# Slot tables of a grouped mixture of experts: the token products move from VectorE to GpSimd, and VectorE makes the one-hots of both halves before its gate products

## The chip, the cores and the metric

The kernel runs on one core of one Trainium2 chip. The metric is the device time of one launch in microseconds, lower is better. The median of the runs is compared, and the profile comes from one execution of its own.

## What is computed

One decoder layer over 2048 tokens of width 1024: a mixer (four mLSTM heads beside gated short convolutions), a LayerNorm, a mixture of sixteen experts with two chosen per token, and a second LayerNorm. The edit is in the mixture. The reference sorts the (token, expert) pairs by expert and lets each expert work on its own rows:

```python
flat_e = expert_idx.reshape(-1)
order = jnp.argsort(flat_e)
tok_sorted = order // TOP_K
gate_sorted = gates.reshape(-1)[order]
...
y = y_buf[dest] * gate_sorted[:, None].astype(x.dtype)
return jnp.zeros_like(xf).at[tok_sorted].add(y).reshape(b, s, d)
```

## The kernel before

The program has four stages, one behind the other with a barrier of all engines between them: the mixer, the router, the experts, the last normalisation. The edit is at the head of the expert stage (the function `experts`).

The router leaves for each of the 4096 pairs (2048 tokens, first and second choice) its expert column, its rank within the expert and its gate. A pair is a place in a tile of 128 partitions x 32: 16 tiles of tokens for the first choice and 16 for the second, which are the two **halves** of this text. From these the expert stage makes **slot tables**: for each of 48 table columns (three for each expert, of 128, 128 and 32 rows) and each of 128 rows, which token sits there, and with what gate. That is a sum over all pairs, and TensorE makes it: for each of the 32 places n, the one-hot of the row (`LOH[:, n]`, 128 wide) is multiplied with `RH[:, n]`, which is 96 wide: the one-hot of the column times the token's number plus one in `RH[:, n, 0]`, and the same one-hot times the gate in `RH[:, n, 1]`. Each fp32 product shows as two passes in the profile, so there are 64 of them (L1680), all added into one PSUM bank.

What VectorE does for that, in `one_hots`, after some short operations on the ranks, is for each half:

1. the column table, `RH[:, half, 1]`: column numbers against a number per pair (L1536), 128x768
2. the row one-hot, `LOH[:, half]` (L1538), 128x2048
3. the token product into `RH[:, half, 0]` (L1541), 128x768
4. the gate product, in place in `RH[:, half, 1]` (L1544), 128x768, which raises `oh_done`

TensorE waits for `oh_done` before place 0 and before place 16. Then VectorE splits the first slice of the first expert's weights (`split_gu(r, 0)`, L1476) and in `tables` reads the sums out of PSUM (L1551 on): the gather rows, which release GpSimd's indirect DMAs of the token rows (L1334), and later the scatter rows. TensorE transposes the gathered rows (L1628), ScalarE and VectorE split them, and the first expert's gate and up products start (L1612).

Each engine has its own queue, written out by hand; what an engine does is in the order of the code. `own.step` counts an operation of VectorE, and `own.wait` waits for all counted ones. `wait_apart` is a wait followed by a carrier that raises another semaphore. GpSimd has nothing between the router's end and the first gather. A loop `Fori(0, n_rounds)` encloses all; it runs once for these inputs. `DVE_TURN` is the number of counted operations in one turn.

Of the kernel before, what the change touches and what calls it, by code (L numbers as in the profile page):

```python
# [7 lines left out]
P = 128  # L8
# [4 lines left out]
ALU = mybir.AluOpType  # L13
# [10 lines left out]
def tensors(nc, ctx, stage):  # L24

    def sb(name, shape, dt=F32):
        return ctx.enter_context(nc.sbuf_tensor(f"{stage}_{name}", shape, dt))

    def ps(name, shape, dt=F32):
        return ctx.enter_context(nc.psum_tensor(f"{stage}_{name}", shape, dt))  # L30

    def sem(name):
        return ctx.enter_context(nc.semaphore(f"{stage}_{name}"))

    return sb, ps, sem


def wait_apart(engine, carrier, sem, value):


    engine.wait_ge(sem, value)
    engine.sem_inc(carrier, 1)
# [28 lines left out]
def mixer(nc, keep, x, w_in, b_in, conv_w, mh_g, w_out, ln_g, ln_b, x1_dram, acc_dram, alpha):  # L71
# [52 lines left out]
    with ctx:  # L124
# [357 lines left out]

        DVE_TURN = 61

        @block.vector
        def _(dve):
            own = Order(dve, dve_own, DVE_TURN)

# [155 lines left out]
            with dve.Fori(0, NG) as g:  # L644
# [88 lines left out]
                for t in range(NT):  # L733
                    dve.scalar_tensor_tensor(out=R[:, t], in0=R[:, t], scalar=lmv[:, t, 0:1], in1=lng[:],
                                             op0=ALU.subtract, op1=ALU.mult).then_inc(ln_gained, 1)
            assert own.n == DVE_TURN, own.n

# [494 lines left out]
def experts(nc, keep, x1_dram, acc_dram, w_gate, w_up, w_down):  # L1232
    D = x1_dram.shape[1]
    NE, _, F = w_gate.shape
    KC = D // P
    FC = F // P
    RING = 3
    NPAIR = keep.pair_rank.shape[1]
    TILES = NPAIR // 2
    NCOL = COLS * NE  # L1240
# [8 lines left out]
    with ctx:  # L1249
        sb, ps, sem = tensors(nc, ctx, "moe")  # L1250
# [11 lines left out]
        slot_f = sb("slot_parts", [P, 2, NPAIR])  # L1262
# [9 lines left out]
        LOH = keep.conv_or_residual[:, 0:NPAIR * P].rearrange("p (n s) -> p n s", s=P)  # L1272
        RH = X[:].rearrange("p k n -> p (k n)")[:, 0:NPAIR * 2 * NCOL].rearrange("p (n a b) -> p n a b", a=2, b=NCOL)
# [11 lines left out]
        dn_h, dn_l = sem("down_high_ready"), sem("down_low_ready")  # L1285
        a_used, b_used, u_used = sem("down_used_by_a"), sem("down_used_by_b"), sem("down_used_by_u")
        oh_done, s_ps = sem("one_hots_ready"), sem("slots_in_psum")
        last_taken, last_ps = sem("last_slots_taken"), sem("last_slots_in_psum")
        gather_ready, scatter_ready = sem("gather_rows_ready"), sem("scatter_rows_ready")
        x_in = [sem(f"x_rows_in{k}") for k in range(COLS)]  # L1290
# [6 lines left out]
        ended, idle = sem("round_ended"), sem("wait_carrier")  # L1297
# [3 lines left out]
        def trips(engine):  # L1301

            return engine.value_load(keep.rounds[0:1, 0:1], min_val=1, max_val=keep.most_rounds)
# [7 lines left out]
        @block.sync  # L1311
        def _(sp):
            n_rounds = trips(sp)
            with sp.Fori(0, n_rounds) as r:
                def load(e, w):
                    sp.wait_ge(gu_l, r * (NE * FC) + e * FC)
                    load_gate_up(sp, keep, w_gate[w], w_up[w])
                    wait_apart(sp, idle, dn_l, r * (NE * 2) + 2 * e)
                    sp.wait_ge(u_used, r * NE + e)
                    load_down(sp, keep, w_down[w])  # L1320

                for e in range(1, NE):
                    load(e, e)
                again = n_rounds - 1 - r
                with sp.If(again):
                    load(NE, 0)
                all_ended(sp, r)

        @block.gpsimd
        def _(pool):  # L1330
            def gather(r, e, k):

                n = ROWS[k]
                pool.indirect_dma_start(out=X[0:n, k], out_offset=None, in_=x1_dram,  # L1334
                                        in_offset=bass.IndirectOffsetOnAxis(
                                            ap=gather_i[0:n, COLS * e + k:COLS * e + k + 1], axis=0))\
                    .then_inc(x_in[k], 16)

            def gather_next(r, e, k):
                if e + 1 < NE:  # L1340
                    wait_apart(pool, idle, x_ps[k], r * NE + e + 1)
                    gather(r, e + 1, k)

            def scatter(r, e, k):
                n = COLS * e + k
                if n:
                    wait_apart(pool, idle, added, r * (NCOL * 16) + n * 16)
                if k == U:
                    wait_apart(pool, idle, yu_done, r * NE + e + 1)
                    to, rows, index = acc_dram.rearrange("s (q n) -> (s q) n", q=QUARTERS), YU[:], last_i[:, e:e + 1]  # L1350
                else:
                    for done in (y_act, y_dve):
                        wait_apart(pool, idle, done, r * (2 * NE) + 2 * e + k + 1)
                    to, rows, index = acc_dram, Y[:, k], scatter_i[:, n:n + 1]
                pool.indirect_dma_start(out=to, out_offset=bass.IndirectOffsetOnAxis(ap=index, axis=0),
                                        in_=rows, in_offset=None, compute_op=ALU.add).then_inc(added, 16)

            n_rounds = trips(pool)
            with pool.Fori(0, n_rounds) as r:
                wait_apart(pool, idle, gather_ready, r + 1)  # L1360
                for k in range(COLS):
                    gather(r, 0, k)
                gather_next(r, 0, A)
                gather_next(r, 0, B)
                wait_apart(pool, idle, scatter_ready, r + 1)
                gather_next(r, 0, U)
                for e in range(NE):
                    gather_next(r, e + 1, A)
                    gather_next(r, e + 1, B)
                    scatter(r, e, A)  # L1370
                    gather_next(r, e + 1, U)
                    scatter(r, e, B)
                    scatter(r, e, U)
                pool.wait_ge(added, r * (NCOL * 16) + NCOL * 16)
                all_ended(pool, r)
# [89 lines left out]

        @block.vector
        def _(dve):
            DVE_TURN = 25 + NE * FC
            own = Order(dve, dve_own, DVE_TURN)

            def split_gu(r, n):
# [41 lines left out]
            def one_hots(r):  # L1513

                def do(instruction):
                    own.step(instruction)
                    own.wait(r)

                rank = keep.pair_rank
                own.step(dve.tensor_scalar(held[:], rank[:], 0.0, None, ALU.is_ge))  # L1520
                own.step(dve.tensor_copy(slot_i[:, 0], rank[:]))
                own.wait(r)
                own.step(dve.scalar_tensor_tensor(out=held[:], in0=rank[:], scalar=float(CAP), in1=held[:],
                                                  op0=ALU.is_lt, op1=ALU.mult))
                own.step(dve.tensor_scalar(slot_i[:, 1], slot_i[:, 0], 7, None, ALU.arith_shift_right))
                do(dve.tensor_scalar(slot_i[:, 2], slot_i[:, 0], P - 1, None, ALU.bitwise_and))
                do(dve.tensor_copy(slot_f[:], slot_i[:, 1:3]))
                do(dve.scalar_tensor_tensor(out=slot_f[:, 0], in0=slot_f[:, 0], scalar=1.0, in1=keep.pair_col[:],
                                            op0=ALU.add, op1=ALU.add))

                do(dve.tensor_tensor(slot_f[:, 0], slot_f[:, 0], held[:], ALU.mult))
                do(dve.tensor_scalar(slot_f[:, 0], slot_f[:, 0], -1.0, None, ALU.add))
                for k in range(2):
                    half = slice(k * TILES, (k + 1) * TILES)
                    of_col, place = (slot_f[:, a, half].unsqueeze(2) for a in (0, 1))
                    own.step(dve.tensor_tensor(RH[:, half, 1], keep.icol[:].unsqueeze(1).to_broadcast([P, TILES, NCOL]),  # L1536
                                               of_col.to_broadcast([P, TILES, NCOL]), ALU.is_equal))
                    own.step(dve.tensor_tensor(LOH[:, half], keep.i128[:].unsqueeze(1).to_broadcast([P, TILES, P]),  # L1538
                                               place.to_broadcast([P, TILES, P]), ALU.is_equal))
                    own.wait(r)  # L1540
                    own.step(dve.tensor_tensor(RH[:, half, 0], RH[:, half, 1],  # L1541
                                               keep.tokp1[:].unsqueeze(2).to_broadcast([P, TILES, NCOL]), ALU.mult))
                    own.wait(r)
                    dve.tensor_tensor(RH[:, half, 1], RH[:, half, 1],  # L1544
                                      keep.pair_gate[:, half].unsqueeze(2).to_broadcast([P, TILES, NCOL]),
                                      ALU.mult).then_inc(oh_done, 1)
# [28 lines left out]
            with dve.Fori(0, n_rounds) as r:  # L1575
# [30 lines left out]
                all_ended(dve, r)  # L1606
            assert own.n == DVE_TURN, own.n

# [290 lines left out]
```

## Time and profile before

| what | us |
|---|---|
| median of 3 runs (1794.78 to 1795.92) | 1795.35 |
| the profiled execution | 1793.36 |
| its span, first to last instruction | 1791.8 |
| TensorE busy | 1638.1 (91%) |
| VectorE busy | 1050.3 (59%) |
| ScalarE busy | 661.3 (37%) |
| GpSimd busy | 344.1 (19%) |

The span is the time from the first to the last instruction of the profiled execution; the time of a launch is 1.6 us longer. A busy share is an average over all stages. In the stretch of the edit, 1012 to 1041 us, the engines hand over to one another and none is busy throughout. The profile names the engines PE (TensorE), DVE (VectorE), ACT (ScalarE), POOL (GpSimd) and SP (SyncE). In a timeline a row is an instruction, or several alike, with its start and duration.

### The profile page before, as it was taken

How to read it: one execution, taken by the hardware profiler on the slowest of the kernel's cores; microseconds unless marked ns; L12 is line 12 of the kernel's file. 1: busy time of each engine (PE TensorE's matmuls, PEld its weight loads, DVE VectorE, ACT ScalarE, POOL GpSimd, SP SyncE). 2: the span in 40 equal slices, each digit the busy share in tenths (PEclk: the TensorE clock that was granted, in tenths of full speed). 3: DMA queues.
4: the chain of work that ended last, by engine and by line, in shares of the span. 5: the costliest groups of instructions: out<-in, count | busy, mean ns of one | idle time of the engine just before them, and what ended most of it. 6: DMA issues, size and time to landing. Idle time of an engine off the chain costs nothing. (4 is left out here: it accounts for less than half of the span.)

```text
span 1791.8 us, 25230 instructions
## 1 busy us (share of the span) xinstructions
PE 1638.1 (91%) x9590; PEld 1424.4 (79%) x9590; DVE 1050.3 (59%) x1572; ACT 661.3 (37%) x938; POOL 344.1 (19%) x236
## 2 busy tenths in 40 slices
PE   8999999999999999999978389999999999999900
PEld 6888888888888888888868388889999999998800
DVE  5446866368663686635865745555555555555448
ACT  3233332243232443324433144444444444444323
POOL 1000033000240002500003012222222222221128
PEclk9999999999999999999998689999999999999955
DMA  7222435224352233532228356666776677766365
GB/s 224 95 79 76 152 119 188 71 71 153 112 183 94 71 119 117 212 94 71 84 86 310 121 171 194 204 199 216 216 210 194 204 217 222 225 211 182 78 206 215
DMA packets 118041, 280.73 MB, mean 157 GB/s; under 512 B 13088, under 2 KB 15136, under 8 KB 117920
## 3 DMA queue, kind: packets, MB, share of 16 engines
q1 hardware_dynamic: 96416, 207.75, 33.9%
q0 software_dynamic: 20928, 69.22, 14.1%
q8 instruction: 82, 1.34, 0.3%
q10 hardware_dynamic: 576, 2.10, 0.3%
q14 instruction: 39, 0.32, 0.1%
HBM read 234.47 MB, written 44.56 MB: 156 GB/s over the span
## 5 line engine op out<-in xcount | busy, mean ns | idle before, releaser
L492 DVE TENSOR_TENSOR mix_w_low<-mix_w_raw,mix_w_high 128x2048 fp32r<-128x2048 f32 x73 | 167.3, 2291 | 164.7 <-ACT mix_w_high L359 164.5
L742 PE MATMUL mix_acc<-mix_xT_high,mix_w_high 128*128 128x512 f32 x640 | 254.2, 397 | 0.7 <-DVE mix_w_low L492 0.7
L744 PE MATMUL mix_acc<-mix_xT_high,mix_w_low 128*128 128x512 f32 x640 | 250.0, 391 | 0.0
L743 PE MATMUL mix_acc<-mix_xT_low,mix_w_high 128*128 128x512 f32 x640 | 249.2, 389 | 0.0
L359 ACT ACTIVATE mix_w_high<-mix_w_raw 128x2048 fp32r<-128x2048 f32 x73 | 139.7, 1913 | 258.1 <-PE mix_acc L744 248.9
L1476 DVE TENSOR_TENSOR moe_gate_up_low<-kept_w_gate_up_raw,moe_gate_up_high 128x2048 fp32r<-128x2048 f32 x64 | 146.6, 2290 | 87.0 <-ACT moe_gate_up_high L1387 87.0
L1612 PE MATMUL moe_gate_psum<-moe_xT_high,moe_gate_up_high 128*128 128x288 f32 x512 | 153.8, 300 | 1.4 <-DVE moe_xT_low L1493 1.4
L1614 PE MATMUL moe_up_psum<-moe_xT_high,moe_gate_up_low 128*128 128x288 f32 x512 | 151.9, 297 | 0.0
L1613 PE MATMUL moe_up_psum<-moe_xT_low,moe_gate_up_high 128*128 128x288 f32 x512 | 151.5, 296 | 0.0
L1613 PE MATMUL moe_gate_psum<-moe_xT_low,moe_gate_up_high 128*128 128x288 f32 x512 | 151.4, 296 | 0.0
L1612 PE MATMUL moe_up_psum<-moe_xT_high,moe_gate_up_high 128*128 128x288 f32 x512 | 151.2, 295 | 0.0
L1614 PE MATMUL moe_gate_psum<-moe_xT_high,moe_gate_up_low 128*128 128x288 f32 x512 | 151.0, 295 | 0.0
L744 PEld LDWEIGHTS mix_acc<-mix_xT_high,mix_w_low 128*128 128x128 f32 x640 | 120.1, 188 | 25.9
L742 PEld LDWEIGHTS mix_acc<-mix_xT_high,mix_w_high 128*128 128x128 f32 x640 | 120.2, 188 | 25.3 <-issue 1.3
L743 PEld LDWEIGHTS mix_acc<-mix_xT_low,mix_w_high 128*128 128x128 f32 x640 | 120.4, 188 | 23.8
L317 POOL DMA_DIRECT2D kept_conv_or_residual<-in_x x16 | 8.4, 528 | 609.5 <-DVE mix_yT_low L552 608.9
L1387 ACT ACTIVATE moe_gate_up_high<-kept_w_gate_up_raw 128x2048 fp32r<-128x2048 f32 x64 | 122.1, 1908 | 0.0
L1334 POOL DMA_INDIRECT moe_x_rows<-x,moe_gather_row x48 | 68.1, 1418 | 263.4 <-PE moe_xT_psum L1628 102.3
L1612 PE MATMUL moe_y_psum<-moe_down_high,moe_hiddenT_high 128*128 128x512 f32 x256 | 103.1, 403 | 7.2 <-DVE moe_y_rows L1510 7.2
L1612 PEld LDWEIGHTS moe_gate_psum<-moe_xT_high,moe_gate_up_high 128*128 128x128 f32 x512 | 96.6, 189 | 7.7 <-issue 7.7
L742 PE MATMUL mix_acc<-mix_w_high,mix_yT_high 128*128 128x512 f32 x256 | 101.5, 396 | 0.0
L1614 PE MATMUL moe_y_psum<-moe_down_high,moe_hiddenT_low 128*128 128x512 f32 x256 | 100.5, 393 | 0.0
(318 smaller groups left out, 3556.0 us busy)
## 6 DMA issues: line engine op xcount, KB each, us to landing
mix_w_raw<-in_w_in SPq DMA_DIRECT2D x57, 1024.0 KB, 5.3
kept_w_gate_up_raw<-in_w_gate SPq DMA_DIRECT2D x32, 1024.0 KB, 8.0
kept_w_gate_up_raw<-in_w_up SPq DMA_DIRECT2D x32, 1024.0 KB, 12.6
kept_w_down_raw<-in_w_down SPq DMA_DIRECT2D x32, 1024.0 KB, 10.0
mix_w_raw<-in_w_out SPq DMA_DIRECT2D x16, 1024.0 KB, 5.2
mix_x_rows<-in_x POOLq DMA_DIRECT2D x16, 512.0 KB, 6.4
kept_conv_or_residual<-in_x POOLq DMA_DIRECT2D x16, 512.0 KB, 5.1
x<-kept_conv_or_residual POOLq DMA_DIRECT2D x16, 512.0 KB, 3.7
```

The costliest lines, as they stand in the source:

```text
L317: pool.dma_start(R[:, t], x[bass.ds(g * GT + t * P, P)]).then_inc(res_in[t], 16)
L359: act.activation(wh[:, stage % 2], raw[:, stage % 2], ACT.Copy).then_inc(split_h, 1)
L492: dve.tensor_tensor(wl[:, stage % 2], raw[:, stage % 2], wh[:, stage % 2].bitcast(F32), ALU.subtract).then_inc(split_l, 1)
L742: pe.matmul(out, ah, bh, start=first, stop=False)
L743: pe.matmul(out, ah, bl, start=False, stop=False)
L744: return pe.matmul(out, al, bh, start=False, stop=last)
L1334: pool.indirect_dma_start(out=X[0:n, k], out_offset=None, in_=x1_dram, in_offset=bass.IndirectOffsetOnAxis(ap=gather_i[0:n, COLS * e + k:C ...
L1387: act.activation(wh[:, n % RING].rearrange("p c k n -> p k c n"), raw_gu[:, :, :, f * P:(f + 1) * P], ACT.Copy).then_inc(gu_h, 1)
L1476: dve.tensor_tensor(wl[:, n % RING].rearrange("p c k n -> p k c n"), raw_gu[:, :, :, f * P:(f + 1) * P], wh[:, n % RING].rearrange("p c k ...
L1612: pe.matmul(out, ah, bh, start=first, stop=False)
L1613: pe.matmul(out, ah, bl, start=False, stop=False)
L1614: return pe.matmul(out, al, bh, start=False, stop=last)
```

## The change

The token products of both halves move to GpSimd, each behind a wait for its half's column table (`columns_found`). VectorE makes both column tables, then both one-hots, then both gate products; each gate product waits for GpSimd's product of its half (`tokens_set`), since it overwrites what GpSimd reads.

```diff
+        columns_found, tokens_set = sem("columns_found"), sem("tokens_set")
...
             with pool.Fori(0, n_rounds) as r:
+                for k in range(2):
+                    half = slice(k * TILES, (k + 1) * TILES)
+                    wait_apart(pool, idle, columns_found, r * 2 + k + 1)
+                    pool.tensor_tensor(RH[:, half, 0], RH[:, half, 1],
+                                       keep.tokp1[:].unsqueeze(2).to_broadcast([P, TILES, NCOL]),
+                                       ALU.mult).then_inc(tokens_set, 1)
                 wait_apart(pool, idle, gather_ready, r + 1)
...
-            DVE_TURN = 25 + NE * FC
+            DVE_TURN = 20 + NE * FC
...
                 for k in range(2):
                     half = slice(k * TILES, (k + 1) * TILES)
-                    of_col, place = (slot_f[:, a, half].unsqueeze(2) for a in (0, 1))
-                    own.step(dve.tensor_tensor(RH[:, half, 1], keep.icol[:].unsqueeze(1).to_broadcast([P, TILES, NCOL]),
-                                               of_col.to_broadcast([P, TILES, NCOL]), ALU.is_equal))
-                    own.step(dve.tensor_tensor(LOH[:, half], keep.i128[:].unsqueeze(1).to_broadcast([P, TILES, P]),
-                                               place.to_broadcast([P, TILES, P]), ALU.is_equal))
-                    own.wait(r)
-                    own.step(dve.tensor_tensor(RH[:, half, 0], RH[:, half, 1],
-                                               keep.tokp1[:].unsqueeze(2).to_broadcast([P, TILES, NCOL]), ALU.mult))
-                    own.wait(r)
+                    dve.tensor_tensor(RH[:, half, 1], keep.icol[:].unsqueeze(1).to_broadcast([P, TILES, NCOL]),
+                                      slot_f[:, 0, half].unsqueeze(2).to_broadcast([P, TILES, NCOL]),
+                                      ALU.is_equal).then_inc(columns_found, 1)
+                for k in range(2):
+                    half = slice(k * TILES, (k + 1) * TILES)
+                    ins = dve.tensor_tensor(LOH[:, half], keep.i128[:].unsqueeze(1).to_broadcast([P, TILES, P]),
+                                            slot_f[:, 1, half].unsqueeze(2).to_broadcast([P, TILES, P]),
+                                            ALU.is_equal)
+                own.step(ins)
+                for k in range(2):
+                    half = slice(k * TILES, (k + 1) * TILES)
+                    dve.wait_ge(tokens_set, r * 2 + k + 1)
                     dve.tensor_tensor(RH[:, half, 1], RH[:, half, 1],
                                       keep.pair_gate[:, half].unsqueeze(2).to_broadcast([P, TILES, NCOL]),
                                       ALU.mult).then_inc(oh_done, 1)
```

VectorE's queue in `one_hots` before, from the first column table to the last gate product (`moe_x_rows` is the buffer that holds RH, `kept_conv_or_residual` the one that holds LOH):

```order
L1536 TENSOR_TENSOR moe_x_rows<-kept_iota_table_column,moe_slot_parts 128x16x48
L1538 TENSOR_TENSOR kept_conv_or_residual<-kept_iota_slot,moe_slot_parts 128x2048
L61 REGISTER_ALU
L1541 TENSOR_TENSOR moe_x_rows<-moe_x_rows,kept_token_plus 128x16x48
L61 REGISTER_ALU
L1544 TENSOR_TENSOR moe_x_rows<-moe_x_rows,kept_pair_gate 128x16x48
L1536 TENSOR_TENSOR moe_x_rows<-kept_iota_table_column,moe_slot_parts 128x16x48
L1538 TENSOR_TENSOR kept_conv_or_residual<-kept_iota_slot,moe_slot_parts 128x2048
L61 REGISTER_ALU
L1541 TENSOR_TENSOR moe_x_rows<-moe_x_rows,kept_token_plus 128x16x48
L61 REGISTER_ALU
L1544 TENSOR_TENSOR moe_x_rows<-moe_x_rows,kept_pair_gate 128x16x48
```

Each half has its four operations together, so the first gate product is the fourth of the eight.

The same place of VectorE's queue in the changed kernel, up to the weight split:

```order
L1542 TENSOR_TENSOR moe_x_rows<-kept_iota_table_column,moe_slot_parts 128x16x48 x2
L1547 TENSOR_TENSOR kept_conv_or_residual<-kept_iota_slot,moe_slot_parts 128x2048 x2
L1553 ISA
L1554 TENSOR_TENSOR moe_x_rows<-moe_x_rows,kept_pair_gate 128x16x48
L1553 REGISTER_ALU
L1554 TENSOR_TENSOR moe_x_rows<-moe_x_rows,kept_pair_gate 128x16x48
L1482 ISA
L1483 TENSOR_TENSOR moe_gate_up_low<-kept_w_gate_up_raw,moe_gate_up_high 128x2x8x128
```

The first gate product is now the fifth operation, behind the second half's table and one-hot; both token products are gone from this queue.

GpSimd's queue at the head of the expert stage in the changed kernel:

```order
L1360 UNCONDITIONAL_BRANCH
L1360 ISA
L1364 TENSOR_TENSOR moe_x_rows<-moe_x_rows,kept_token_plus 128x16x48
L41 REGISTER_ALU
L1364 TENSOR_TENSOR moe_x_rows<-moe_x_rows,kept_token_plus 128x16x48
L41 REGISTER_ALU
L1335 DMA moe_x_rows<-x,moe_gather_row 128x1024 x2
L1335 DMA moe_x_rows<-x,moe_gather_row 32x1024
```

The two products stand ahead of the three first gathers, which before were the first thing that GpSimd did in this stage.

## Rows read from the trace of the kernel before

**Rows 1.** The page: the span, and TensorE's busy time, share and instructions.
```profile
span 1791.8 us, 25230 instructions
PE 1638.1 (91%) x9590; PEld 1424.4 (79%) x9590; DVE 1050.3 (59%) x1572; ACT 661.3 (37%) x938; POOL 344.1 (19%) x236
```

**Rows 2.** The waits of TensorE, 1045 to 1735 us: total, times, longest.
```profile
PE moe_y_psum L1612 <- DVE moe_y_rows L1510: 7.2, 16, 1.0
```

**Rows 3.** The timeline of VectorE and TensorE, 1012 to 1041 us: start, duration.
```profile
1012.60 0.96 DVE L1536 TENSOR_TENSOR moe_x_rows<-kept_iota_table_column,moe_slot_parts 128x768 f32<-128x768 f32 x1
1013.48 2.29 DVE L1538 TENSOR_TENSOR kept_conv_or_residual<-kept_iota_slot,moe_slot_parts 128x2048 f32<-128x2048 f32 x1
1015.79 0.96 DVE L1541 TENSOR_TENSOR moe_x_rows<-moe_x_rows,kept_token_plus 128x768 f32<-128x768 f32 x1
1016.79 0.96 DVE L1544 TENSOR_TENSOR moe_x_rows<-moe_x_rows,kept_pair_gate 128x768 f32<-128x768 f32 x1
1017.66 0.95 DVE L1536 TENSOR_TENSOR moe_x_rows<-kept_iota_table_column,moe_slot_parts 128x768 f32<-128x768 f32 x1
...
1017.80 9.96 PE L1680 MATMUL moe_y_psum<-moe_x_rows,kept_conv_or_residual 128*128 128x96 f32 x64 [14.32 <-DVE moe_x_rows L1544]
1018.53 2.28 DVE L1538 TENSOR_TENSOR kept_conv_or_residual<-kept_iota_slot,moe_slot_parts 128x2048 f32<-128x2048 f32 x1
1020.85 0.96 DVE L1541 TENSOR_TENSOR moe_x_rows<-moe_x_rows,kept_token_plus 128x768 f32<-128x768 f32 x1
1021.84 0.96 DVE L1544 TENSOR_TENSOR moe_x_rows<-moe_x_rows,kept_pair_gate 128x768 f32<-128x768 f32 x1
1022.72 2.28 DVE L1476 TENSOR_TENSOR moe_gate_up_low<-kept_w_gate_up_raw,moe_gate_up_high 128x2048 fp32r<-128x2048 f32 x1
1027.80 0.21 DVE L1551 TENSOR_SCALAR moe_slot_token<-moe_y_psum 128x48 f32<-128x48 f32 x1 [2.79 <-PE moe_y_psum L1680]
...
1033.53 1.94 PE L1628 MATMUL moe_xT_psum<-kept_identity,moe_x_rows 128*128 128x128 f32 x8 [4.76 <-DMA moe_x_rows<-x,moe_gather_row]
...
1040.48 0.60 PE L1612 MATMUL moe_gate_psum<-moe_xT_high,moe_gate_up_high 128*128 128x288 f32 x1 [1.43 <-DVE moe_xT_low L1493]
```

**Rows 4.** Windows, the table passes alone (L1680): length, TensorE busy (started), clock.
```profile
core 0: us, PE busy (x) PEld busy (x), PEclk, DMA share, GB/s
1017.70:1023.20 5.50, 5.40 (x25) 5.40 (x26) 0.50 0.00 0
1017.70:1024.00 6.30, 6.20 (x32) 6.20 (x33) 0.56 0.00 0
1017.70:1027.80 10.10, 9.96 (x64) 9.79 (x64) 0.73 0.00 0
```

**Rows 5.** The timeline of the final normalisation: one operation of each engine alone.
```profile
1735.03 1.17 DVE L1815 TENSOR_TENSOR norm_normed<-norm_normed,norm_ln_gain 128x1024 f32<-128x1024 f32 x1
...
1786.40 2.33 POOL L1824 TENSOR_TENSOR norm_normed<-norm_normed,norm_ln_bias 128x1024 f32<-128x1024 f32 x1
```

**Rows 6.** The timeline, 1776 to 1785 us: both engines' queues full.
```profile
1776.47 1.21 DVE L1815 TENSOR_TENSOR norm_normed<-norm_normed,norm_ln_gain 128x1024 f32<-128x1024 f32 x1
...
1776.63 3.25 POOL L1824 TENSOR_TENSOR norm_normed<-norm_normed,norm_ln_bias 128x1024 f32<-128x1024 f32 x1 [1.16 <-DVE norm_normed L1815]
...
1777.61 3.36 DVE L1815 TENSOR_TENSOR norm_normed<-norm_normed,norm_ln_gain 128x1024 f32<-128x1024 f32 x1
...
1779.85 3.31 POOL L1824 TENSOR_TENSOR norm_normed<-norm_normed,norm_ln_bias 128x1024 f32<-128x1024 f32 x1
...
1780.89 3.35 DVE L1815 TENSOR_TENSOR norm_normed<-norm_normed,norm_ln_gain 128x1024 f32<-128x1024 f32 x1
```

**Rows 7.** The timeline of the router stage, 943 to 947 us.
```profile
943.89 2.37 POOL L980 TENSOR_TENSOR kept_conv_or_residual<-kept_conv_or_residual,kept_ln_bias 128x1024 f32<-128x1024 f32 x1
944.90 1.51 DVE L1097 TENSOR_TENSOR route_router_w_low<-route_router_w,route_router_w_high 128x128 fp32r<-128x128 f32 x1 [7.52 <-ACT route_router_w_high L1017]
```

**Rows 8.** VectorE's groups by line and form: busy, mean ns of one.
```profile
L1141 DVE TENSOR_TENSOR route_pair_high<-route_logits 128x128 f32<-128x128 f32 x1 | 0.3, 291 | 0.0
```

## The prediction

> **What bounds the kernel now.** I first read the page: TensorE is busy for 91% of the span [rows 1]. Then the waits of TensorE over the sixteen experts, from 1045 to 1735 us: one group, 7.2 us in all, and none of it on a load or on GpSimd [rows 2]. So the expert stage runs at TensorE's own pace, and whatever delays its start is added to the end nearly in full. The edit lies just ahead of it, in the stretch in which the slot tables are made. There the timeline of VectorE and TensorE [rows 3] is the view to read. VectorE runs eight tensor_tensors without a break from 1012.60 us: for each half a column table (0.96 us), a one-hot (2.29 us), a token product (0.96 us) and a gate product (0.96 us). TensorE begins at 1017.80 us, 0.05 us after the first half's gate product ends. The second half is ready at 1022.80 us (1021.84 + 0.96).
>
> Which half sets TensorE's end? Its 64 passes are 32 for each half. By the windows [rows 4] 25 had started by 1023.20 us at a granted clock of 0.50 (the level of 1.2 GHz), and the 32nd only by 1024.00 us. The second half had then been ready for 1.2 us. So TensorE never waits for it: **the start of the first half's work sets the end**, and the second half has slack. Behind the passes come the table reads on VectorE at 1027.80 us, the gathers, the transposes at 1033.53 us and the first expert at 1040.48 us [rows 3], a chain with nothing beside it that could take over.
>
> **What the change does to that chain.** VectorE's new order is both column tables, both one-hots, then both gate products; the two token products run on GpSimd. The first gate product now stands behind two more operations, the other half's table and one-hot, and its own token product has gone to the other engine.
>
> If GpSimd and VectorE did not disturb each other, the sum would be short. The second column table is put ahead (0.88 us from start to start, 1012.60 to 1013.48 [rows 3]), the second one-hot too (2.20 us: 2.29 less the 0.08 by which an unwaited successor starts early), and the first token product goes (1.00 us, 1015.79 to 1016.79). About 0.1 us of gaps goes with the waits. That is 0.88 + 2.20 - 1.00 - 0.10 = +2.0 us on TensorE's start, even with the products for nothing.
>
> They are not for nothing. I looked at how GpSimd's tensor_tensors and VectorE's ones with two inputs in SBUF run side by side. A GpSimd addition of 128x1024 takes 2.33 us alone and VectorE's product of that size 1.17 us alone [rows 5]. Where both queues are full they take 3.31 and 3.35 us [rows 6], and the ends fit a strict turn-taking: VectorE ends at 1780.97 (1777.61 + 3.36), GpSimd at 1783.16 (1779.85 + 3.31), VectorE at 1784.24 (1780.89 + 3.35). Each gets 2.19 or 1.08 us after the other's end; they do not overlap. The router stage shows the same: a VectorE operation of 128x128 which elsewhere takes 0.29 us [rows 8] took 1.51 us, and ended 0.15 us after GpSimd's addition (943.89 + 2.37 = 946.26) [rows 7]. A queued GpSimd operation also got its turn although VectorE's next operation was queued too (GpSimd's at 1776.63 against VectorE's at 1777.61 [rows 6]).
>
> The Trainium skill has this as a rule against the change: in "SBUF — State Buffer", section "Who interferes with whom", a VectorE instruction with two SBUF inputs contends with a GpSimd instruction that reads SBUF, and the later one blocks fully. By that rule the trace agrees: 1.51 us in place of 0.29. Without the rule and the rows the sum would be +2.0 us.
>
> VectorE's tables, one-hots and gate products all have both inputs in SBUF, and so have GpSimd's products. **The price of a product**, seen by VectorE, is then 2.19 us x 768/1024 = 1.64 us. Its lower end is 0 (no exclusion) and its upper end 2.19 us, what the larger operation took, since the row operand is broadcast here and no row of GpSimd shows that. I take 1.64, because type and engine are those of the rows and only the length differs. The page "GPSIMD Engine Reference", section "3.1 Elementwise — side-by-side cycle accounting", of the Trainium skill gives 4497 ns for 2048 elements; as an estimate from that page a product is 1.69 us whole, about 1.55 us after the handover, and the sum 0.2 us less.
>
> The chain, step by step:
> - column tables 1012.60 to 1013.56 and 1013.48 to 1014.43. GpSimd is idle and is released by the first, so its product is queued before the second table ends
> - first token product: 1014.43 + 1.64 = 1016.07
> - first one-hot, after GpSimd's end 0.09 us shorter than 2.29 (as 1.08 to 1.17): + 2.19 = 1018.26
> - second token product, queued meanwhile: 1019.90
> - second one-hot: 1022.09
> - first gate product from 1022.01 (0.08 early) to 1022.97. Nothing of GpSimd's is left to contend
> - TensorE starts at 1023.02, against 1017.80: **+5.2 us**
>
> If GpSimd wakes too late for the turn after the second table, it takes the turns after the two one-hots instead; the same two products still stand ahead of the gate product, and the sum is the same. The second gate product ends at 1023.85, and TensorE needs it some 6 us after its start (32 passes, 1017.80 to 1024.00), so it is covered. VectorE's weight split of 2.28 us (from 1022.72) moves to about 1023.8 to 1026.1; it now ends 2.8 us before the table reads and would end 6.9 us before them. GpSimd's queue behind the products is the first gather, due some 13 us after them, and it waits for the tables anyway. No DMA is moved past another; SP's queue is untouched. ScalarE has its weight split there and waits for nothing that moves within it. Four waits of VectorE on itself go (the 0.1 us above); its two new waits for GpSimd are met by 1016.07 and 1019.90, before the gate products come up, and cost nothing as long as the products end by then.
>
> The profiled execution took 1793.36 us (span 1791.8 and 1.6 around it), so it would give 1798.6. It lies 2.0 us under the median of the runs shown; against that median of 1795.35 the forecast is **1800.6 us**.
>
> **What is uncertain besides.** The clock. In the trace it stayed at 0.50 until some 5.4 us after TensorE's start, 25 passes, and the other 39 took 4.6 us [rows 4]: 0.216 us a pass at the low level and 0.117 us at the high one. I let the same delay follow the later start. All passes at the high level would give 2.5 us back (64 x 0.117 = 7.5 against 9.96); all at the low one cost 3.9 us more (13.8). The first expert starts at the low clock too, so shifting it can add or save a part of that again.
>
> **The rivals.**
> - *No exclusion for these operations.* For: the rows are of plain 1024-wide operands, not of broadcasts. Against: the 0.29 us operation that took 1.51. Then +2.0 us, 1797.4, within the resolution. This is the way to "not slower"; it decides where the products cost VectorE less than 0.8 us each, half of 3.6 - 2.0. Chance 0.10.
> - *The clock gives it back.* TensorE starts 5.2 us later and the clock is up from its first passes: 5.2 - 2.5 = +2.7, 1798.1. The passes ran at 0.50 at first [rows 4], behind 14.32 us without work [rows 3], and that idle time only grows. Chance 0.08.
> - *The product is dear.* Broadcast costs GpSimd its way up to 2.19 us: + 1.1, 1801.7; the page's rule on its pace speaks for none of that. Chance 0.08.
> - *The second half was the bound.* With products for nothing it would be ready 2.15 us earlier (1020.65), 1793.2, still within the resolution. The count of 25 passes at 1023.20 speaks against it, and with exclusion the half is later, not earlier. Chance 0.02.
>
> **How the numbers follow.** The forecast has 0.72. A measurement of this kernel can tell about 0.2%, 3.6 us, from no change; the bound lies at 1798.9, and +5.2 clears it by 1.6 us, less than the clock can move. I give nine tenths of the forecast's chance and all of the dear product's to slower, 0.73; 0.25 to the same; 0.02 to faster, which no case reaches except by noise. The range runs from the rival without exclusion, 1797.2, to the dear product with a part of the clock's cost, 1803.2.
>
> **What the profile would show.** Right: two GpSimd tensor_tensors with spans over 2 us between 1013.6 and 1020; one-hots on VectorE that look like 3.9 us in place of 2.29; TensorE's first pass near 1023.0; the expert stage unchanged in length. Wrong: one-hots that keep 2.29 us, with TensorE at 1019.8, would fell the exclusion; TensorE waiting in the middle of its passes would fell the slack of the second half; a difference that arises after 1041 us would mean that the end does not follow this chain.

## The result and the profile after

The changed kernel takes 1798.38 us in the median of 19 runs (1795.26 to 1801.04), the kernel before 1793.94 us in the median of 19 runs beside it (1791.43 to 1797.28). The ratio is 1.0022, 95% interval 1.0015 to 1.0029: slower by 4.4 us between the medians, 3.9 us by the ratio, 2.7 to 5.2 us by its interval. The profiled execution has a span of 1796.0 us, 4.2 more than before [rows 1].

The page of that execution:

```profile
span 1796.0 us, 25232 instructions
...
PE 1635.0 (91%) x9590; PEld 1421.1 (79%) x9590; DVE 1050.1 (58%) x1570; ACT 660.9 (37%) x938; POOL 348.2 (19%) x238
```

VectorE has two instructions fewer and GpSimd two more. VectorE's busy time did not fall, 1050.1 us against 1050.3, although 1.9 us of products went from it: a first sign that its other operations became longer.

The stretch of the edit next, as the timeline shows it in the changed kernel, each operation by itself:

```profile
1011.25 0.96 DVE L1542 TENSOR_TENSOR moe_x_rows<-kept_iota_table_column,moe_slot_parts 128x768 f32<-128x768 f32 x1
...
1012.12 0.95 DVE L1542 TENSOR_TENSOR moe_x_rows<-kept_iota_table_column,moe_slot_parts 128x768 f32<-128x768 f32 x1
...
1012.39 2.02 POOL L1364 TENSOR_TENSOR moe_x_rows<-moe_x_rows,kept_token_plus 128x768 f32<-128x768 f32 x1 [54.22 <-DVE moe_x_rows L1542]
...
1012.99 3.56 DVE L1547 TENSOR_TENSOR kept_conv_or_residual<-kept_iota_slot,moe_slot_parts 128x2048 f32<-128x2048 f32 x1
...
1014.37 3.51 POOL L1364 TENSOR_TENSOR moe_x_rows<-moe_x_rows,kept_token_plus 128x768 f32<-128x768 f32 x1
...
1016.48 3.55 DVE L1547 TENSOR_TENSOR kept_conv_or_residual<-kept_iota_slot,moe_slot_parts 128x2048 f32<-128x2048 f32 x1
...
1019.95 0.94 DVE L1554 TENSOR_TENSOR moe_x_rows<-moe_x_rows,kept_pair_gate 128x768 f32<-128x768 f32 x1
```

These answer to [rows 3]. The one-hots, 2.29 us before, now show 3.56 and 3.55 us, and the products are in the gaps: the second table ends at 1013.07 (1012.12 + 0.95), the first product at 1014.41, the first one-hot at 1016.55, the second product at 1017.88, the second one-hot at 1020.03. Each end is behind that of the other engine by 1.33 to 1.34 us for a product and 2.14 or 2.15 us for a one-hot. Nothing overlaps. Read an operation's cost from end to end here: of the first one-hot's 3.56 us, 1.42 us (1012.99 to 1014.41) are its wait for GpSimd's product, and of the second product's 3.51 us, 2.18 us (1014.37 to 1016.55) are its wait for the one-hot. These waits lie inside the spans, so the profile counts them as busy time of both engines.

Then TensorE and the reads behind it, in the same timeline:

```profile
1020.95 9.30 PE L1690 MATMUL moe_y_psum<-moe_x_rows,kept_conv_or_residual 128*128 128x96 f32 x64 [18.82 <-DVE moe_x_rows L1554]
1021.69 2.28 DVE L1483 TENSOR_TENSOR moe_gate_up_low<-kept_w_gate_up_raw,moe_gate_up_high 128x2048 fp32r<-128x2048 f32 x1
1030.30 0.21 DVE L1561 TENSOR_SCALAR moe_slot_token<-moe_y_psum 128x48 f32<-128x48 f32 x1 [6.33 <-PE moe_y_psum L1690]
...
1043.24 0.60 PE L1622 MATMUL moe_gate_psum<-moe_xT_high,moe_gate_up_high 128*128 128x288 f32 x1 [1.43 <-DVE moe_xT_low L1500]
```

From the first table's start to TensorE's first pass it was 5.20 us before and is 9.70 us now: **+4.5**. VectorE itself got nothing out of the move: its last gate product ends 10.51 us after the first table starts (1019.95 + 1.81, two of them, less 1011.25), where it took 10.20 us. Its idle time ahead of the table reads grew from 2.79 to 6.33 us, because these reads wait for TensorE and come 19.05 us after the first table, 15.20 before. The windows of TensorE show the clock (columns as in [rows 4]; the first two are of the changed kernel's table passes alone):

```profile
1020.80:1024.90 4.10, 3.95 (x18) 3.95 (x19) 0.50 0.00 0
1020.80:1030.30 9.50, 9.30 (x64) 9.14 (x64) 0.78 0.00 0
```

and at the start of the first expert, all work, in the changed kernel (busy TensorE, its weight loads, VectorE, ScalarE, GpSimd, then the clock):

```profile
1043.20:1048.80 5.60, 5.56 (x23) 5.57 (x24) 2.29 (x1) 2.11 (x2) 0.53 (x1) 0.50 0.41 120
1048.90:1049.90 1.00, 1.00 (x9) 1.00 (x9) 0.00 (x0) 0.00 (x0) 0.00 (x0) 1.00 0.00 0
```

against the kernel before:

```profile
1040.40:1043.60 3.20, 3.11 (x13) 3.12 (x14) 2.29 (x1) 2.16 (x2) 0.58 (x1) 0.50 0.70 205
```

So the low level (0.50, the 1.2 GHz one) lasted 4.05 us into the table passes, where it had lasted 5.4 us, and 5.7 us into the first expert, where it had lasted 3.2 us. The ledger of the two profiled executions, in us:

| part | before | after | difference |
|---|---|---|---|
| span's start to the first table | 1012.60 | 1011.25 | -1.35 |
| first table to TensorE's first pass | 5.20 | 9.70 | +4.50 |
| the 64 passes | 9.96 | 9.30 | -0.66 |
| to the first expert's first product | 12.72 | 12.99 | +0.27 |
| from there to the end of the span | 751.3 | 752.8 | +1.4 |
| sum | 1791.8 | 1796.0 | +4.2 |

The first line has no part in the change; it varies from execution to execution (the first table starts between 1010.50 and 1013.65 us in the profiles shown below). The 0.27 us are for the most part a longer wait of TensorE for the second gather (0.90 us, 0.66 before). The last line is mostly the longer low clock: 2.4 us more at half the clock hold back about 1.2 us of work, and TensorE's busy time in the expert stage is 1.0 us longer for the same 4712 products. Without the first line the profile would show +5.5 us, so that its 4.2 us lie so near the medians' 4.4 us is in part chance. The waits in the expert stage are what they were [rows 2], word for word but for the line numbers:

```profile
PE moe_y_psum L1622 <- DVE moe_y_rows L1517: 7.2, 16, 1.0
```

### The profile page after: what moved, and what is told of

Read it like the earlier page. It is cut to its first block and busy times, and to the rows that moved or that the text cites. A ratio compares the mean times of both kernels' runs of the same rounds, so it can differ in the third digit from the quotient of the medians.

```text
span 1796.0 us, 25232 instructions
## 1 busy us (share of the span) xinstructions
PE 1635.0 (91%) x9590; PEld 1421.1 (79%) x9590; DVE 1050.1 (58%) x1570; ACT 660.9 (37%) x938; POOL 348.2 (19%) x238
## 3 DMA queue, kind: packets, MB, share of 16 engines
q8 instruction: 82, 1.34, 0.3%
```

## The experiments

The theory: VectorE's operations with two inputs in SBUF and GpSimd's products take turns, each holding the other off for its whole length; what is slower is TensorE's start, and that is handed on to the end. The rivals: the one-hots became long by their order or the missing waits; GpSimd and VectorE do not exclude each other; the second part was the bound. The quantity in all of them is the time from the first table's start to TensorE's first pass (the interval, in what follows), which one profile shows to 0.01 us, while single runs of one kernel scatter by some 6 us. The first four kernels were timed in one sequence against 33 runs of the kernel before (median 1794.15), the last three against 21 (1794.49).

### The changed order, all on VectorE

Against the changed kernel, in the main:

```diff
-                    wait_apart(pool, idle, columns_found, r * 2 + k + 1)
-                    pool.tensor_tensor(RH[:, half, 0], RH[:, half, 1],
-                                       keep.tokp1[:].unsqueeze(2).to_broadcast([P, TILES, NCOL]),
-                                       ALU.mult).then_inc(tokens_set, 1)
...
+                own.wait(r)
+                for k in range(2):
+                    half = slice(k * TILES, (k + 1) * TILES)
+                    own.step(dve.tensor_tensor(RH[:, half, 0], RH[:, half, 1],
+                                               keep.tokp1[:].unsqueeze(2).to_broadcast([P, TILES, NCOL]), ALU.mult))
+                own.wait(r)
```

Both products stand on VectorE between the one-hots and the gate products.

> The changed order of the operations, with the token products kept on VectorE (both tables, both one-hots, both token products, both gate products). Measured from the start of the first column table to TensorE's first pass: 5.20 us in the kernel before, 9.70 us in the changed one. Theory, that VectorE and GpSimd take turns: one-hots of 2.29 us again (3.56 in the changed kernel) and an interval of about 8.9 us, so moving the products to GpSimd cost 0.8 us more than keeping them; against the kernel before +3.5 us. Rival, that the one-hots became longer by their order or by the missing waits: they stay near 3.5 us here and the interval is over 10 us.

The timeline of this kernel:

```profile
1011.96 1.82 DVE L1536 TENSOR_TENSOR moe_x_rows<-kept_iota_table_column,moe_slot_parts 128x768 f32<-128x768 f32 x2
1013.70 4.48 DVE L1541 TENSOR_TENSOR kept_conv_or_residual<-kept_iota_slot,moe_slot_parts 128x2048 f32<-128x2048 f32 x2
1018.22 1.83 DVE L1547 TENSOR_TENSOR moe_x_rows<-moe_x_rows,kept_token_plus 128x768 f32<-128x768 f32 x2
...
1021.09 9.33 PE L1688 MATMUL moe_y_psum<-moe_x_rows,kept_conv_or_residual 128*128 128x96 f32 x64 [18.26 <-DVE moe_x_rows L1552]
```

Both one-hots together take 4.48 us, where they took 7.04 (1012.99 to 1020.03) beside GpSimd. The interval is 9.13 us (8.9 expected); 1798.64 us, ratio 1.0020 (1.0011 to 1.0029). This order, with nothing on GpSimd, is thus worth +3.9 us on TensorE's start: the second half's table (0.9 us), its one-hot (2.2) and its token product (0.9) now stand ahead of the first gate product. Moving the products to GpSimd adds another 0.6 (0.8 expected): they hold VectorE up for 2 x 1.33 us there and take 1.83 us on its own queue, and 0.2 us come back since the two one-hots end 2.14 us after GpSimd, where they need 4.48 us for both here. The rival that blamed the one-hots' order falls. The total times of this kernel and of the changed one do not differ within their intervals, so the 0.6 us is shown by the profiles alone.

### The products on GpSimd, the order as before

The changed kernel with its three loops over the halves made one, so that a half's table, one-hot and gate product stand together:

```diff
                     dve.tensor_tensor(RH[:, half, 1], keep.icol[:].unsqueeze(1).to_broadcast([P, TILES, NCOL]),
...
-                for k in range(2):
-                    half = slice(k * TILES, (k + 1) * TILES)
-                    ins = dve.tensor_tensor(LOH[:, half], keep.i128[:].unsqueeze(1).to_broadcast([P, TILES, P]),
+                    own.step(dve.tensor_tensor(LOH[:, half], keep.i128[:].unsqueeze(1).to_broadcast([P, TILES, P]),
...
-                own.step(ins)
-                for k in range(2):
-                    half = slice(k * TILES, (k + 1) * TILES)
                     dve.wait_ge(tokens_set, r * 2 + k + 1)
```

> The products on GpSimd, but half by half as in the kernel before: table, one-hot, gate product, and only then the second half. Turn-taking: the first one-hot holds the port already when GpSimd's product is queued, so the product shows a span of some 3.4 us and ends 1.33 us after the one-hot; TensorE starts 5.5 us after the first table starts (5.20 before), and the time is that of the kernel before within 1 us. Rival without exclusion: the product is done before the one-hot ends, the gate product follows at once, 4.15 us to TensorE's start and 1 us faster than before.

```profile
1013.03 0.96 DVE L1542 TENSOR_TENSOR moe_x_rows<-kept_iota_table_column,moe_slot_parts 128x768 f32<-128x768 f32 x1
1013.91 2.28 DVE L1545 TENSOR_TENSOR kept_conv_or_residual<-kept_iota_slot,moe_slot_parts 128x2048 f32<-128x2048 f32 x1
1014.17 3.35 POOL L1364 TENSOR_TENSOR moe_x_rows<-moe_x_rows,kept_token_plus 128x768 f32<-128x768 f32 x1 [54.93 <-DVE moe_x_rows L1542]
...
1017.56 0.96 DVE L1549 TENSOR_TENSOR moe_x_rows<-moe_x_rows,kept_pair_gate 128x768 f32<-128x768 f32 x1 [1.36 <-POOL moe_x_rows L1364]
...
1018.57 9.83 PE L1685 MATMUL moe_y_psum<-moe_x_rows,kept_conv_or_residual 128*128 128x96 f32 x64 [14.66 <-DVE moe_x_rows L1549]
```

Here the one-hot started first and keeps its 2.28 us; now it is the product that shows 3.35 us, 1.33 of them behind the one-hot's end at 1016.19. The same exclusion, with the long row on the other engine. The interval is 5.54 us; 1794.55 us, ratio 1.0001 (0.9992 to 1.0010). With the order undone the loss is gone, though the products stay on GpSimd: the order is the main cost. The rival without exclusion, 4.15 us and 1 us faster than before, falls, and the move gains nothing because the product does not run beside the one-hot.

### The slot numbers in PSUM

```diff
+                own.step(dve.tensor_copy(pg[1][:, 0:P], keep.i128[:]))
...
-                    ins = dve.tensor_tensor(LOH[:, half], keep.i128[:].unsqueeze(1).to_broadcast([P, TILES, P]),
+                    ins = dve.tensor_tensor(LOH[:, half], pg[1][:, 0:P].unsqueeze(1).to_broadcast([P, TILES, P]),
```

> The changed kernel with the slot numbers copied into PSUM ahead, so that each one-hot has a single input in SBUF. Theory, that only operations with two inputs in SBUF exclude GpSimd: the one-hots take about 2.3 us beside GpSimd's products, the interval from the first table to TensorE's start falls from 9.70 to about 7.2 us, and the time to +2 us against the kernel before. Rival, that any VectorE operation that reads SBUF takes turns with GpSimd, or that the one-hots are long for another reason: the interval stays at 9.7 us.

```profile
1013.65 1.82 DVE L1543 TENSOR_TENSOR moe_x_rows<-kept_iota_table_column,moe_slot_parts 128x768 f32<-128x768 f32 x2
1014.79 3.45 POOL L1364 TENSOR_TENSOR moe_x_rows<-moe_x_rows,kept_token_plus 128x768 f32<-128x768 f32 x2 [55.50 <-DVE moe_x_rows L1543]
1015.39 4.48 DVE L1548 TENSOR_TENSOR kept_conv_or_residual<-moe_gate_psum,moe_slot_parts 128x2048 f32<-128x2048 f32 x2
...
1020.79 10.25 PE L1691 MATMUL moe_y_psum<-moe_x_rows,kept_conv_or_residual 128*128 128x96 f32 x64 [16.45 <-DVE moe_x_rows L1555]
```

Order and engines are those of the changed kernel, and only one input of the one-hots has another home. They are back at 4.48 us for both, 2.28 us each, with both products done beside them by 1018.24; the second of these took 1.47 us. The interval is 7.14 us; 1796.90 us, ratio 1.0014 (1.0005 to 1.0024). This is the experiment that names the cause of the long one-hots: it is the second input in SBUF that excludes GpSimd.

### The first gate product ahead of the second one-hot

The changed kernel with the loops of the one-hots and of the gate products made one; the tables stay ahead:

```diff
-                    ins = dve.tensor_tensor(LOH[:, half], keep.i128[:].unsqueeze(1).to_broadcast([P, TILES, P]),
+                    own.step(dve.tensor_tensor(LOH[:, half], keep.i128[:].unsqueeze(1).to_broadcast([P, TILES, P]),
...
-                own.step(ins)
-                for k in range(2):
-                    half = slice(k * TILES, (k + 1) * TILES)
                     dve.wait_ge(tokens_set, r * 2 + k + 1)
```

> The changed kernel with the first gate product ahead of the second half's one-hot (tables, first one-hot, first gate product, second one-hot, second gate product). Turn-taking: the second token product takes the turn after the first one-hot although VectorE's gate product is queued and does not need it, so the interval is 1.83 + 1.33 + 2.14 + 1.33 + 0.87 = about 7.55 us, and the time +2.3 us against before. Without turn-taking (VectorE keeps the port while it has work queued) about 6.2 us; with no exclusion 4.95 us and faster than before.

```profile
1010.59 1.83 DVE L1542 TENSOR_TENSOR moe_x_rows<-kept_iota_table_column,moe_slot_parts 128x768 f32<-128x768 f32 x2
1011.74 5.50 POOL L1364 TENSOR_TENSOR moe_x_rows<-moe_x_rows,kept_token_plus 128x768 f32<-128x768 f32 x2 [52.41 <-DVE moe_x_rows L1542]
1012.34 3.56 DVE L1547 TENSOR_TENSOR kept_conv_or_residual<-kept_iota_slot,moe_slot_parts 128x2048 f32<-128x2048 f32 x1
1015.82 2.22 DVE L1551 TENSOR_TENSOR moe_x_rows<-moe_x_rows,kept_pair_gate 128x768 f32<-128x768 f32 x1
...
1018.10 9.84 PE L1687 MATMUL moe_y_psum<-moe_x_rows,kept_conv_or_residual 128*128 128x96 f32 x64 [16.62 <-DVE moe_x_rows L1551]
```

The gate product shows 2.22 us instead of 0.94: it stood in VectorE's queue when the one-hot ended at 1015.90, and the second token product, which it does not need, ran until 1017.24. So VectorE does not keep its turn by having work queued. That product had been asked for earlier, at about 1013.7 us, and the gate product at 1015.82: in this case's rows whatever ran next had also waited longer, so strict turn-taking and the order of asking can't be told apart. The interval is 7.51 us; 1796.96 us, ratio 1.0017 (1.0008 to 1.0026).

### A plain operand for GpSimd

```diff
+        wide = hT[:].rearrange("p c n -> p (c n)")[:, 0:TILES * NCOL].rearrange("p (n b) -> p n b", b=NCOL)
...
-                                       keep.tokp1[:].unsqueeze(2).to_broadcast([P, TILES, NCOL]),
+                                       wide,
```

`wide` is filled by one copy of VectorE at the head of `one_hots`.

> The changed kernel with the token numbers written out as a plain 128x768 operand, ahead of everything, so that GpSimd's products read no broadcast. The product took 1.33 us of the port in the changed kernel, where 1.64 had been forecast from plain operands of 1024. Theory, that the broadcast made it cheap: now 1.64 us each, one-hots of about 3.85 us, and 10.3 us from the first table to TensorE's start (9.70 with the broadcast). Rival, that the shorter length did: 1.33 us and 9.7 us as before. The added copy (under 1 us) lies ahead of the interval and is in the time: changed kernel +1 to +1.6 us.

```profile
1010.50 1.83 DVE L1544 TENSOR_TENSOR moe_x_rows<-kept_iota_table_column,moe_slot_parts 128x768 f32<-128x768 f32 x2
...
1011.64 2.34 POOL L1365 TENSOR_TENSOR moe_x_rows<-moe_x_rows,moe_hiddenT 128x768 f32<-128x768 f32 x1 [53.16 <-DVE moe_x_rows L1544]
...
1012.24 3.89 DVE L1549 TENSOR_TENSOR kept_conv_or_residual<-kept_iota_slot,moe_slot_parts 128x2048 f32<-128x2048 f32 x1
...
1016.06 3.88 DVE L1549 TENSOR_TENSOR kept_conv_or_residual<-kept_iota_slot,moe_slot_parts 128x2048 f32<-128x2048 f32 x1
...
1020.86 9.81 PE L1692 MATMUL moe_y_psum<-moe_x_rows,kept_conv_or_residual 128*128 128x96 f32 x64 [19.96 <-DVE moe_x_rows L1556]
```

The second table ends at 1012.33 (two of 1.83 us from 1010.50) and the product at 1013.98: 1.65 us, against 1.33 with the broadcast. The interval is 10.36 us (10.3 expected); 1800.61 us in four runs, ratio 1.0041 (1.0026 to 1.0057). That is 2.2 us over the changed kernel's median, where 1 to 1.6 was expected; four runs from 1796.46 to 1803.57 us do not settle such a difference.

### Quarters instead of halves, on VectorE

```diff
-                for k in range(2):
-                    half = slice(k * TILES, (k + 1) * TILES)
+                for k in range(4):
+                    half = slice(k * PART, (k + 1) * PART)
...
-                    if n % TILES == 0:
-                        pe.wait_ge(oh_done, r * 2 + n // TILES + 1)
+                    if n % PART == 0:
+                        pe.wait_ge(oh_done, r * 4 + n // PART + 1)
```

The kernel before with its four operations made for eight places at a time.

> The kernel before with its four operations made for a quarter of the pairs at a time (8 places), all on VectorE. Theory, that TensorE's start sets the end and the later parts have slack: TensorE starts some 2.85 us after the first table starts (5.20 before), the passes then wait a little for the last quarter (ready at about 11.2 us), and the table reads come some 2 us earlier than before; time 2 us less than before (ratio 0.9989). Rival, that the last part was already the bound: nothing gained or slower by the seven added fixed costs of VectorE's operations, some 0.5 us.

```profile
1013.47 0.56 DVE L1537 TENSOR_TENSOR moe_x_rows<-kept_iota_table_column,moe_slot_parts 128x384 f32<-128x384 f32 x1
...
1016.41 10.80 PE L1681 MATMUL moe_y_psum<-moe_x_rows,kept_conv_or_residual 128*128 128x96 f32 x64 [12.06 <-DVE moe_x_rows L1545]
...
1024.16 0.56 DVE L1545 TENSOR_TENSOR moe_x_rows<-moe_x_rows,kept_pair_gate 128x384 f32<-128x384 f32 x1
...
1027.25 0.21 DVE L1552 TENSOR_SCALAR moe_slot_token<-moe_y_psum 128x48 f32<-128x48 f32 x1 [0.33 <-PE moe_y_psum L1681]
```

and the windows of its table passes:

```profile
1016.30:1023.50 7.20, 7.09 (x33) 7.09 (x34) 0.50 0.00 0
1016.30:1024.70 8.40, 8.29 (x43) 8.29 (x44) 0.57 0.00 0
```

TensorE starts 2.94 us after the first table (5.20 before), yet the table reads come 13.78 us after it, 1.4 us earlier than before and not 2: the passes took 10.80 us, since the clock stayed low for 7.2 us of them. It was not the last quarter: that was ready at 1024.72, when 43 of 64 passes had started and the 49th would be the first to need it. 1792.52 us, ratio 0.9988 (0.9979 to 0.9997): faster than before. The smaller parts cost VectorE 1.05 us in all, where 0.5 was expected (the last gate product ends 11.25 us after the first table starts, 10.20 before), and it had that to spare.

### Quarters, with the products on GpSimd and the slot numbers in PSUM

The edits of the quarters and of the slot numbers in PSUM together, with the changed kernel's products on GpSimd for a quarter each. On VectorE a quarter's table, one-hot and gate product stand together.

> Quarters, the token products on GpSimd, and the slot numbers in PSUM so that the one-hots do not exclude GpSimd. Theory: each product runs beside its quarter's one-hot, TensorE starts about 2.3 us after the first table, every quarter is ready before TensorE needs it (each takes 2.2 us of VectorE against 3.4 us of TensorE at the low clock), and the table reads follow the first table by 2.3 + 9.9 = 12.2 us (15.2 before); with the 0.3 us of the copy ahead, 2.6 us less than before (ratio 0.9985), 0.6 us less than the quarters on VectorE alone. Rival, that GpSimd's fixed cost on the smaller product outlasts the one-hot: the gate products wait, and it is no better than the quarters alone.

```profile
1012.23 0.56 DVE L1544 TENSOR_TENSOR moe_x_rows<-kept_iota_table_column,moe_slot_parts 128x384 f32<-128x384 f32 x1
1012.71 1.22 DVE L1547 TENSOR_TENSOR kept_conv_or_residual<-moe_gate_psum,moe_slot_parts 128x1024 f32<-128x1024 f32 x1
1012.97 0.83 POOL L1365 TENSOR_TENSOR moe_x_rows<-moe_x_rows,kept_token_plus 128x384 f32<-128x384 f32 x1 [54.79 <-DVE moe_x_rows L1544]
1013.84 0.55 DVE L1551 TENSOR_TENSOR moe_x_rows<-moe_x_rows,kept_pair_gate 128x384 f32<-128x384 f32 x1
...
1014.45 9.22 PE L1687 MATMUL moe_y_psum<-moe_x_rows,kept_conv_or_residual 128*128 128x96 f32 x64 [11.53 <-DVE moe_x_rows L1551]
```

Now the product does run beside the one-hot: 0.83 us, over at 1013.80, with the one-hot at its own 1.22 us until 1013.93. TensorE starts 2.22 us after the first table and the table reads come 11.47 us after it. Of the 2.31 us by which these reads are earlier than with the quarters on VectorE, 0.72 is TensorE's start; the other 1.58 are the passes (9.22 for 10.80 us), that is, the clock of these two executions. 1791.81 us, ratio 0.9985 (0.9976 to 0.9994). It is the fastest of those run and beats the kernel before and the changed one; that it beats the quarters alone is not shown, since the intervals overlap.

## Why the prediction was right

- *The start of the first half sets the end.* Right. The ledger shows +4.50 at that place and the waits of the expert stage unchanged. The intervals of the nine kernels from 2.22 to 10.36 us order their ratios without an exception; between the medians only the changed order on VectorE and the change itself stand the other way round, by 0.1 us.

| kernel | first table to TensorE, us | median less the kernel before, us | ratio |
|---|---|---|---|
| quarters, GpSimd, PSUM | 2.22 | -2.7 | 0.9985 |
| quarters on VectorE | 2.94 | -2.0 | 0.9988 |
| before | 5.20 | 0 | 1 |
| products on GpSimd, old order | 5.54 | +0.4 | 1.0001 |
| slot numbers in PSUM | 7.14 | +2.8 | 1.0014 |
| gate product earlier | 7.51 | +2.8 | 1.0017 |
| changed order on VectorE | 9.13 | +4.5 | 1.0020 |
| the change | 9.70 | +4.4 | 1.0022 |
| plain operand | 10.36 | +6.1 | 1.0041 |

- *The order alone: +2.0 us with the products for nothing.* Right. The slot numbers in PSUM hide the products beside the one-hots, and the interval then was 7.14 us, 1.94 over that before. So of the +4.50 us 1.94 are the order, less the product that left VectorE's queue, and 2.56 the two products that VectorE waits for (9.70 less 7.14).
- *The exclusion and the turn-taking.* Right, from rows of two other stages; only that it was the turn and not the order of asking which decided was more than those rows, or any here, can show. The Trainium skill's "SBUF — State Buffer", section "Who interferes with whom", has a VectorE instruction with two SBUF inputs contend with a GpSimd instruction that reads SBUF, and one with at most one SBUF input, outside the 2-port modes, not. The trace agrees: beside GpSimd's products a one-hot took 3.56 us with two inputs in SBUF and 2.28 us with one of them in PSUM.
- *The price of a product, 1.64 us.* This is the term that was mis-sized: 1.33 us. Scaling by length was right for a plain operand (1.65 us measured), but one operand is a broadcast, and that made it cheaper, where the prediction only allowed for dearer. Two products make 0.62 us of the 0.72 by which the chain was overrated (+5.22 against +4.50); the handovers of the one-hots (2.14 and not 2.19) make the rest.
- *The clock follows TensorE's start with the same delay.* Not so in the single profile: the low level ended 1.4 us sooner in the passes and 2.4 us later in the first expert. Nor do the other profiles show such an order: with TensorE's start at 5.20 us after the first table the low level lasted 5.4 us in the passes and 3.2 in the first expert, at 9.70 us 4.05 and 5.7, at 10.36 us 5.0 and 2.8. The rival that the clock gives 2.5 us back did not come true: the passes gave 0.66 back, and the first expert took more than that. What the clock does to the median can't be told, since the ratio's interval runs from 2.7 to 5.2 us.
- *The signs named.* Two products with spans over 2 us (2.02 and 3.51), long one-hots (3.56 us, 3.9 forecast), no wait inside the passes and an expert stage without new waits: as named. TensorE's first pass at 1020.95 rather than 1023.0 is 1.35 us of an earlier start of the stretch and 0.72 us of the overrated chain.
- *The size.* 1800.6 was forecast as the old median plus 5.2; the difference measured is 4.4, close to the resolution of 3.6. The other 1.4 us of the gap to 1798.38 is the kernel before, whose median fell from 1795.35 to 1793.94 with more runs. The lower bound of the range, 1797.2, is 0.2 us under the sum of the rival that it is taken from (1795.35 + 2.0); nothing hangs on it.

What stays open is what sets the moment at which the clock rises; no run here varied that by itself.

## What to carry to other kernels

Before work goes from VectorE to GpSimd, look at what VectorE does meanwhile: beside its operations with two inputs in SBUF, GpSimd's product, which reads SBUF, saved nothing and cost its own, longer, duration (1.33 us for 0.96); with one input of the one-hots in PSUM the two ran together. Where TensorE waits for several parts of a table and is the slower one, order the work by the first part alone, and make that part small. Batching like operations of all parts moves the first result behind work that had slack.

## What the runs showed of the hardware

- A GpSimd product of 128x768 held VectorE off for 1.33 us with one operand broadcast along its inner dimension and for 1.65 us with that operand plain, the kernels being alike but for the copy that writes it out.
- Once both engines had work queued they changed turns with every operation: GpSimd's second product ran ahead of a waiting gate product (2.22 us for 0.94). It had also been asked for earlier than the gate product.
- The exclusion shows in whichever row started second: the one-hot at 3.56 us in one kernel, the product at 3.35 us beside a one-hot of 2.28 us in the other.
- The granted clock stayed at 0.50 for some 3.8 to 7.2 us after TensorE's first table pass in the nine profiles (3.8 with the quarters on GpSimd, 4.05 in the changed kernel, 5.4 before, 7.2 with the quarters on VectorE), which moves the duration of the same 64 passes between 9.22 and 10.80 us.
